# Low parts of the first feed-forward weights: added by transfers instead of subtracted on VectorE

## What is computed

```python
u = _rmsnorm(h, norm_ffn_g[l])
up = _dwconv(u @ w_up[l], ffn_conv_w[l], ffn_conv_b[l])
a_half, v_half = jnp.split(up, 2, axis=-1)
h = h + (jax.nn.silu(a_half) * v_half) @ w_down[l]
```

## Time and profile before

| | |
|---|---|
| time, median of 2 runs | 2102.34 us (2100.99 to 2103.68) |
| profiled execution, span | 2098.0 us (4.3 us under the median) |
| PE busy | 1965.0 us, 94% |
| DVE busy | 1271.7 us, 61% |
| ACT busy | 932.0 us, 44% |
| POOL busy | 31.4 us, 1% |
| read from DRAM | 495.38 MB, 237 GB/s over the span |

### The profile page before, as it was taken

How to read it: one execution, slowest core, us unless ns; L and a number is a source line. 1 busy time by engine, 2 the same in 40 slices (tenths; PEclk the granted TensorE clock), 3 DMA queues, 4 the chain that set the end, 5 groups by cost and what they waited for, 6 DMA issues and landing times.

```text
span 2098.0 us, 45360 instructions
## 1 busy us (share of the span) xinstructions
PE 1965.0 (94%) x19452; PEld 1719.3 (82%) x19452; DVE 1271.7 (61%) x2183; ACT 932.0 (44%) x1166; POOL 31.4 (1%) x62
## 2 busy tenths in 40 slices
PE   8999999999999999999999999999999996777776
PEld 7998869999999999988689999999977764444444
DVE  6887879489688567896895796786435311111111
ACT  5544655574565445546455754664422310111011
POOL 0000000000000000000000000000000000000000
PEclk9999999999999999999999999999999998999988
DMA  6555344445455554654434544555777899999997
GB/s 238 183 206 188 130 161 143 170 181 187 167 183 184 205 184 160 218 202 147 176 129 154 201 161 163 186 186 190 264 321 277 353 427 429 429 428 429 429 429 318
DMA packets 60269, 498.86 MB, mean 238 GB/s; under 512 B 7152, under 2 KB 7280, under 8 KB 12240
## 3 DMA queue, kind: packets, MB, share of 16 engines
q1 hardware_dynamic: 54864, 479.57, 59.5%
q0 software_dynamic: 4384, 14.49, 2.1%
q10 hardware_dynamic: 864, 2.49, 0.4%
HBM read 495.38 MB, written 1.15 MB: 237 GB/s over the span
## 4 chain that ended last, share of the span: by engine, by line
PE 72%; DMA 15%; DVE 8%; ACT 3%; issue 1%; ACTq 0%; SPq 0%; DVEq 0%
PE bank L1063 28%; DMA arena<-stream 15%; PE bank L1068 14%; PE bank L1073 4%; PE bank L1670 3%; PE bank L1051 3%; PE bank L1357 3%; PE bank L1002 3%; PE bank L990 2%; PE bank L1056 1%; DVE ring_r L2742 1%; PE bank L1105 1%; PE bank L1704 1%; PE bank L1649 1%; PE bank L1460 1%
## 5 line engine op out<-in xcount | busy, mean ns | idle before, releaser
L2742 DVE TENSOR_TENSOR ring_r<-ring,weights_and_u_split 128x2048 fp32r<-128x2048 f32 x88 | 201.5, 2291 | 76.5 <-ACT weights_and_u_split L2050 72.8
L1068 PE MATMUL bank<-weights_and_u_split,ring_r 128*128 128x256 f32 x1880 | 246.4, 283 | 0.0
L1068 PEld LDWEIGHTS bank<-weights_and_u_split,ring_r 128*128 128x128 f32 x1880 | 234.8, 192 | 0.0
L1063 PE MATMUL bank<-weights_and_u_split,hidden_and_weights_high 128*128 128x256 f32 x1664 | 211.5, 284 | 0.0
L1063 PEld LDWEIGHTS bank<-weights_and_u_split,hidden_and_weights_high 128*128 128x128 f32 x1664 | 203.6, 192 | 4.8 <-issue 4.3
L2050 ACT ACTIVATE weights_and_u_split<-ring 128x2048 fp32r<-128x2048 f32 x88 | 167.6, 1906 | 53.8 <-PE bank L1068 42.4
L3103 DVE COPY arena<-bank 128x128 f32<-128x128 f32 x32 | 9.3, 292 | 287.1 <-PE bank L1688 287.1
L1670 PE MATMUL bank<-arena 128*32 128x256 f32 x1504 | 108.5, 439 | 62.3 <-DMA arena<-stream 61.3
L2742 DVE TENSOR_TENSOR ring_r<-ring,hidden_and_weights_high 128x2048 fp32r<-128x2048 f32 x64 | 146.2, 2287 | 28.6 <-ACT hidden_and_weights_high L2050 28.5
L2239 ACT ACTIVATE arena<-bank 64x256 f32<-64x256 f32 x32 | 12.1, 377 | 314.1 <-PE bank L1670 314.1
L1670 PEld LDWEIGHTS bank<-arena 128*32 128x32 f32 x1504 | 54.7, 122 | 111.0 <-issue 51.5
(11 more groups left out here) (487 smaller groups left out, 3630.1 us busy)
## 6 DMA issues: line engine op xcount, KB each, us to landing
ring<-stream SPq DMA_DIRECT2D x267, 1024.0 KB, 4.8
arena<-stream SPq DMA_DIRECT2D x55, 2048.0 KB, 25.7
ring<-stream SPq DMA_DIRECT2D x26, 2048.0 KB, 26.7
arena<-stream SPq DMA_DIRECT2D x19, 1024.0 KB, 10.9
arena<-rows_scratch POOLq DMA_DIRECT2D x48, 256.0 KB, 4.2
place_of_rows<-stream SPq DMA_DIRECT2D x2, 1024.0 KB, 6.0
place_of_parameters<-stream SPq DMA_DIRECT2D x2, 1024.0 KB, 8.0
h<-x_d ACTq DMA_DIRECT2D x4, 256.0 KB, 4.9
```

Source lines behind the costliest of these rows:

```text
L1063: pe.matmul(bank[:, c * S:(c + 1) * S], whi[k][:, c * P:(c + 1) * P], yhi[k] if xx is None else xx[:, k, :], start=(sub == 0 and c == part ...
L1068: mm = pe.matmul(bank[:, c * S:(c + 1) * S], wlo[k][:, c * P:(c + 1) * P], yhi[k] if xhi is None else xhi[:, k, :], start=False, stop=(end ...
L2742: tt(scan_high_or_low(k, ring_r[:, POS[k] % RING, :]), scan_high_or_low(k, w), high(k).bitcast(F32), ALU.subtract)\
```

## The change

For the 44 up units the parts change places. ACT writes the negated high part into the buffer. POOL then issues a transfer that reads the unit from DRAM once more and adds it onto that buffer, which so becomes the low part. DVE no longer subtracts: it rounds the raw slot in place, which gives the high part. PE takes its high weights from the slot and its low weights from the buffer: it waits for DVE ahead of the first pass, and for the landing of the transfer ahead of the low pass. The landings count on the semaphores of the spread rows, so the counts that DVE waits for there are adapted. All other split weights (`SPLIT` without `ADDED`) stay as they were.

```diff
+ADDED = [n for n in SPLIT if KINDS[n] == "up"]
+ADDED_IN = [[n for n in ADDED if POS[n] % RING == r] for r in range(RING)]
...
+        def spread_landed(lay, r, nth):
+
+            return bc_in[r], 16 * (lay * (SPREADS + len(ADDED_IN[r])) + nth)
+
+        def low_landed(lay, n):
+
+            r = POS[n] % RING
+            return spread_landed(lay, r, SPREADS + ADDED_IN[r].index(n) + 1)
...
+                for n in ADDED:
+                    pool.wait_ge(whi_ok.sem, whi_ok.at(lay, NTH_SPLIT[n] + 1))
+                    pool.dma_start(high(n), stream[lay * UNITS + POS[n]], accum_op=ALU.add).then_inc(bc_in[POS[n] % RING], 16)
...
-                if n in NTH_SPLIT:
+                if n in ADDED:
+                    pe.wait_ge(wlo_ok.sem, wlo_ok.at(lay, NTH_SPLIT[n] + 1))
+                elif n in NTH_SPLIT:
...
+                    low = (wlo_ok.sem, wlo_ok.at(lay, NTH_SPLIT[n] + 1))
+                    if n in ADDED:
+                        whi, wlo, low = wlo, whi, low_landed(lay, n)
...
-                    pe.wait_ge(wlo_ok.sem, wlo_ok.at(lay, NTH_SPLIT[n] + 1))
+                    pe.wait_ge(*low)
...
-                    act.activation(high(k), scan_high_or_low(k, ring[:, POS[k] % RING, :]), ACT.Copy).then_inc(whi_ok.sem, 1)
+                    act.activation(high(k), scan_high_or_low(k, ring[:, POS[k] % RING, :]), ACT.Copy,
+                                   scale=-1.0 if k in ADDED else 1.0).then_inc(whi_ok.sem, 1)
...
+                    if k in ADDED:
+                        V.tensor_copy(ring_r[:, POS[k] % RING, :], w).then_inc(wlo_ok.sem, 1)
+                        return
```

## The result

The change makes the kernel slower, by 3.4%:

| | before | after |
|---|---|---|
| time, median of 2 runs | 2102.34 us | 2172.78 us (2172.10 to 2173.46) |
| ratio after / before, 95% interval | | 1.0336 (1.0306 to 1.0366) |
| span of the profiled execution | 2098.0 us | 2170.3 us |
| mean granted clock of TensorE | 0.981 | 0.979 |

A forecast was written before the change was run, and what follows sets the result against it. PE's matmuls were taken to bound the up stage, then the oversubscribed DMA engines: 29.9 us lost a layer, 60 us for two, on 2098 gives 2158 us of span, plus 4.3 us to the median, 2162 us; range 2097 to 2265 us.

The forecast's parts named there:

- the forecast one: Up stages: an adding transfer costs two passes (A about 3.9 to 5.9 us) or latency binds, 2120 to 2204 us; chance 0.46.
- The bound, and the gain of 0: Up stage: PE's own matmuls bound it, so replacing 44 DVE subtractions (101 us of DVE time) by casts gains 0.
- The moved wait, 0: PE's first pass in up units waits for DVE's rounding instead of ACT's copy; covered by 5.7 us, cost 0.
- A, 4.9 us: DMA engines' time for one 1 MB adding transfer: two passes over its bytes, 4.9 us, between 2.45 and 7.35 us.
- The sum: Up stage: 21 accumulations (102.9 us) and some 20 loads (49 us) delay the last low pass by 29.9 us a layer.
- Nothing won back behind the stage: The stages behind the up stage are bound by PE again, so nothing of the loss is won back.
- Hidden: Rival: an accumulation takes the DMA engines no more than 3.5 us, PE stays at 5.76 us a unit, 2102 us; chance 0.27.
- Slower than two passes: Rival: an adding transfer's reads and write do not overlap; 2225 us at 6.4 us, 2265 us at 7.35 us; chance 0.25.
- Latency: Rival: landings over 11.9 us make the three high buffers bind, about 23 us a layer, 2148 us; chance counted with the forecast.
- DVE in POOL's way: Rival: DVE's operation delays POOL's issue by at most 2.29 us, hidden except for up1, under 1 us; no chance given.
- from up4 or so: Sign in the up stage: the unit from which PE would wait before its low pass for a transfer into the weights' buffers.
- nothing up to A = 3.5 us: Threshold: a layer loses 21 × A - 73 us, so an adding transfer of up to 3.5 us of DMA time costs nothing.

The follow-up runs named there:

- e8: The changed kernel with DVE's rounding done by a two-input maximum (2.29 us) in place of the cast (1.23 us): 2173.67 us, ratio 1.0351 to the kernel before.
- e2: The changed kernel with two plain copies on POOL's queue in place of each adding transfer: 2173.26 us, ratio 1.0347 to the kernel before.
- e1: The changed kernel with 44 plain copies on POOL's queue in place of the adding transfers: 2104.55 us, ratio 1.0021 to the kernel before.
- e6: The changed kernel with the ring's slot given back after the second pass, not after the low pass: 2172.53 us, ratio 1.0348 to the kernel before.
- e3: The change for every second up unit only, the others split as in the kernel before: 2132.64 us, ratio 1.0160 to the kernel before.
- e7: Every second up unit by adding transfer, as e3, with the ring's slot given back before the low pass: 2120.02 us, ratio 1.0097 to the kernel before.
- e9: The change for every third up unit only, 7 additions in a layer: 2108.02 us, ratio 1.0037 to the kernel before.

## Why the prediction was right

The time lay in the range, 10.8 us above the 2162 us, and the case was the forecast one. Its steps:

- **The bound, and the gain of 0.** Right. DVE's operation became 1.23 us, well inside the bounds of 0 and 2.29 us, and PE gained nothing; e8 gives the DVE time back and the kernel takes as long.
- **The moved wait, 0.** Right: among PE's waits from 540 to 1600 us none is for DVE's cast (L2764).
- **A, 4.9 us.** Right in kind, a little low. It measures 5.05 us, two passes to within 3%, and e2 shows that two passes is what it is. The rule that I weighed there (the Trainium skill, Collectives: The Full Stack, "The bandwidth ceiling: the fold count and why AG ≠ RS ≠ AR") has 1.93 as the measured ratio of an all-gather's bandwidth to that of a reduce-scatter, and puts it down to the two source reads of the add; the trace agrees for this transfer, with 1.94 between an addition and a load. What was off in my figure was the base, 2.45 us, the price of a load in the last stage: in this one it is 2.60 us.
- **The sum.** Right in form, low in its terms. The last low pass began at 713.60 us, where I had 707.2. From up1's issue at 552.7 us to that pass the queues' own counts are 22.02 MB of additions at a share of 66.2% and 22.96 MB of loads at 35.6%: 21 additions take 106.5 us (I had 102.9) and 21.9 loads 57.3 us (I had 20, and 49 us). The loads beyond my count are up3's, which was issued only at 551.9 us, and more of the down weights. The two terms were low by 11.9 us in all. That the sum missed by 6.4 us only is in part luck: the start that I put too late and the landing's tail, 1.3 us each, and the 2.9 us by which the packets' times, 163.8 us, exceed the 160.9 us that passed, go the other way. So a layer lost 36.3 us (713.60 against 677.34 us), not 29.9; the second layer lost as much (its last low pass begins at 1506.34 us, before at 1433.91, 72.4 us in all), and this is the whole 72.3 us of span.
- **Nothing won back behind the stage.** Right, as the last 644 us show.
- **Hidden.** Fell: A is 5.05 us, not 3.5. e1 is what this rival would have looked like, since a plain second read does hide.
- **Slower than two passes.** Fell: the row that spoke for it, POOL's queue at its present efficiency, was that of short rows. Under full load the copies of e2, with rows of 8 KB, cost 2.58 us for a transfer of 1 MB on the same queue (68.9% of 120 us for 32.1 of them), not 3.2.
- **Latency.** I counted it with the forecast as alike in sign and size. For the whole change e6 decides against it. For half of the units (e3) a loop takes a part, by e7, in a form that I had not thought of: not the three buffers, but the ring's loop of load, copy, addition and low pass.
- **DVE in POOL's way.** There, but small: 0.22 us for each issue, and covered. The Trainium skill (SBUF — State Buffer, "A bandwidth-pool intuition that's wrong (but worth ruling out)") has such a transfer wait until DVE's copy ends and some 115 ns more; the trace agrees with that, with 0.11 us behind the cast's end. The 2.5 us that I took from its example do not carry over: the hold ends with the cast, which is 1.23 us long here.
- **Signs that I had wrong.** The waits begin at up1, not "from up4 or so": three slots were loaded when the stage began, not four, and up1's addition shared the engines with 1.2 MB of loads (552 to 563 us) and landed 10.1 us after its issue, where 8.9 us were free from the copy's end. The landing is 12.9 us, not 8 to 11, since I did not let queueing into it; the loads were late by the same cause. POOL's issue is 0.87 to 1.16 us, not 0.54. The first of the three is also in the sum, as up3's load; the other two did not carry it, since it went by the engines' time.

The step that fails in a smaller change is the threshold "nothing up to A = 3.5 us". It asks only whether the engines' mean demand fits PE's time. e3 has a mean demand of 5.05 / 2 + 2.60 = 5.1 us a unit by the prices of the changed kernel, and of 5.4 us by its own (addition 5.45 us, load 2.71 us), both under 5.76, and lost 1.6%, where e1 with the same work by count lost 0.2%.

## What to carry to other kernels

Price an adding transfer at two copies of its bytes in DMA engines' time, wherever its second operand lies, and set that against the room that the engines have in that very stage. Time saved on an engine that nobody waits for buys nothing, so moving it to a resource that is half used already can at best cost nothing. And a mean share under 1 is not enough: add up the landings, copies and passes that a ring's slot goes through, as queues lengthen them in the longest turns and not in the median one, and compare with what the consumer takes for as many units as the ring has slots.

## What was not expected of the hardware

The DMA engines' time for the same megabyte is not one number. An addition takes 5.05 us in the changed kernel (share 1.03), 5.45 us in e3 (0.87), 5.70 us in e9 (0.79; 30.5% of 120 us for 6.42 units) and 5.8 us for the first one of the changed kernel (48.4% of the 12 us from 540 to 552). A load takes 2.45 us in the last stage, 2.60 us in the changed kernel, 3.0 us in the kernel before (0.52 of 5.76 us). In most of these rows the price is higher where the share is lower, but not in all: a load takes 3.11 us in e7 at 0.96. Since the shares of the changed kernel add up to over 1, the times of packets overlap, so a share counts more than the engines' own work, and a share near 1 can still hold some reserve: e1 is full by that measure (0.96), moves 357 GB/s where e2 moves 421, and costs PE 0.2%.

```profile
q0 software_dynamic: 934, 6.73, 30.5%
```

```profile
q0 software_dynamic: 144, 1.05, 48.4%
```

(POOL's queue in e9 from 560 to 680 us, and in the changed kernel from 540 to 552 us: packets, MB, share of 16 engines' time.)

Issuing an adding transfer takes POOL 0.86 us with no hold by the cast (e8), where the plain issue that stood clear of a cast in e1 took 0.53 us.

PE's clock falls after some waits and not after others. In e3 PE waited for 2.31 us ahead of the low pass at 601.58 us, which took 3.55 us, and the granted clock of that slice of 20 us was 0.91; in the changed kernel it waited for 2.43 us ahead of the one at 594.13 us, which took 2.18 us. No run here shows what decides. In the kernel before the same stage had 1.00 at 120.00 us of 120.00 busy.
